# Second block's second mixer: latent projections ahead of the indexer, weight slabs split by quarters, and the last selection steps between attention steps

## The reference, cut to what matters

```python
def odd_mixer(x, w_in, q_norm_g, kv_norm_g, w_uq, w_ukv, w_o):
    qc, kc, vc, qi, ki, wi, cq, ckv, kr = split_cols(x @ w_in, ODD_SIZES)
    out_c = dsa_attention(qc, kc, vc, qi, ki, wi)          # 8 heads, 1 kv head
    q  = (rms_norm_2(cq, q_norm_g) @ w_uq)                 # rank 256 -> 8 x (64 + 32)
    kv = (rms_norm_2(ckv, kv_norm_g) @ w_ukv)              # rank 128 -> 8 x (64 + 64)
    ...                                                    # rope on q's and k's last 32
    out_d = causal_block_attention(q, k, kv[..., MLA_NOPE:])
    return jnp.concatenate([out_c, out_d], axis=-1) @ w_o
```

## Time and profile before

| | |
|---|---|
| median of 3 runs | 2633.47 us (2627.46 to 2636.49) |
| the profiled execution | 2608.53 us, its span 2606.3 us |
| mean granted TensorE clock in it | 0.949 of 2.4 GHz |
| PE busy | 2456.7 us, 94% of the span |
| DVE, ACT busy | 1716.4 us (66%), 1190.4 us (46%) |
| the mixer that is changed | from 2041 us to about 2240 us of the span |

### The profile page before, as it was taken

How to read it: one execution, slowest core, us unless ns; L and a number is a source line. 1 busy time by engine, 2 the same in 40 slices (tenths; PEclk the granted TensorE clock), 3 DMA queues, 4 the chain that set the end, 5 groups by cost and what they waited for, 6 DMA issues and landing times.

```text
span 2606.3 us, 33935 instructions
## 1 busy us (share of the span) xinstructions
PE 2456.7 (94%) x14244; PEld 2104.4 (81%) x14244; DVE 1716.4 (66%) x2226; ACT 1190.4 (46%) x1482; POOL 98.7 (4%) x187
## 2 busy tenths in 40 slices
PE   6999999898989999999999999899899879899998
PEld 2778887767789999998899988677778757778776
DVE  4897776654766656655466555587788653588786
ACT  3212222343544444445254444376576433476665
POOL 0111111010000000000000000000000000000000
PEclk8999999999999999999899998999999865999999
DMA  7677877322134544554344542287788310298774
GB/s 269 212 242 263 267 264 248 122 89 76 65 116 176 195 164 176 194 202 178 107 165 169 194 152 81 69 298 278 269 335 328 121 65 17 86 354 309 290 302 183
DMA packets 80385, 501.17 MB, mean 192 GB/s; under 512 B 9604, under 2 KB 10708, under 8 KB 28496
## 3 DMA queue, kind: packets, MB, share of 16 engines
q1 hardware_dynamic: 59120, 423.66, 44.4%
q0 software_dynamic: 21088, 75.01, 9.2%
HBM read 497.58 MB, written 1.05 MB: 191 GB/s over the span
## 4 chain that ended last, share of the span: by engine, by line
PE 69%; DVE 16%; ACT 9%; issue 4%; DMA 2%; DVEq 0%; SPq 0%; ACTq 0%
PE bank L394 67%; DVE wl L1896 7%; ACT wh L1301 6%; DVE macc L1929 2%; PE bank L577 1%; ACT s L1389 1%; DVE f L2054 1%; DMA raw<-in_wstream 1%; DVE s L2045 1%; PE bank L1198 1%; DMA raw<-in_wmod 1%; DVE rs L1953 1%; DVE hl L2029 0%; ACT H L1398 0%; ACT X L1624 0%
## 5 line engine op out<-in xcount | busy, mean ns | idle before, releaser
L1896 DVE TENSOR_TENSOR wl<-raw,wh 128x2048 fp32r<-128x2048 f32 x393 | 899.2, 2290 | 409.3 <-ACT wh L1301 407.2
L1301 ACT ACTIVATE wh<-raw 128x2048 fp32r<-128x2048 f32 x393 | 750.0, 1911 | 379.1 <-PE bank L394 363.3
L394 PE MATMUL bank<-hh,wh 128*128 128x258 f32 (+2 forms) x2200 | 703.8, 320 | 37.2 <-DVE wl L1896 18.8
L394 PE MATMUL bank<-hh,wl 128*128 128x258 f32 (+2 forms) x2200 | 683.7, 311 | 0.0
L394 PE MATMUL bank<-hl,wh 128*128 128x258 f32 (+2 forms) x2200 | 682.2, 310 | 0.0
L394 PEld LDWEIGHTS bank<-hh,wh 128*128 128x128 f32 x2200 | 430.7, 196 | 66.5 <-issue 19.0
L394 PEld LDWEIGHTS bank<-hl,wh 128*128 128x128 f32 x2200 | 431.2, 196 | 18.6
L394 PEld LDWEIGHTS bank<-hh,wl 128*128 128x128 f32 x2200 | 429.8, 195 | 19.0
L394 PE MATMUL bank<-wh,hh 128*128 128x512 f32 (+1 forms) x704 | 278.4, 395 | 5.1 <-DVE hl L2804 2.8
L394 PE MATMUL bank<-wl,hh 128*128 128x512 f32 (+1 forms) x704 | 274.1, 389 | 0.0
L394 PE MATMUL bank<-wh,hl 128*128 128x512 f32 (+1 forms) x704 | 273.8, 389 | 0.0
(11 more groups left out here) (424 smaller groups left out, 2709.8 us busy)
## 6 DMA issues: line engine op xcount, KB each, us to landing
raw<-in_wstream SPq DMA_DIRECT2D x393, 1024.0 KB, 4.9
mring<-in_wmod POOLq DMA_DIRECT2D x128, 512.0 KB, 4.6
raw<-in_wmod SPq DMA_DIRECT2D x8, 1024.0 KB, 9.7
X<-in_xT SPq DMA_DIRECT2D x1, 2048.0 KB, 12.6
bias<-in_nabias POOLq DMA_DIRECT2D x16, 128.0 KB, 2.5
c_sglg<-in_sglg POOLq DMA_DIRECT2D x1, 1024.0 KB, 5.0
c_sglb<-in_sglb POOLq DMA_DIRECT2D x1, 1024.0 KB, 7.4
out<-X SPq DMA_DIRECT2D x4, 256.0 KB, 2.2
```

The costliest lines, as they stand in the source:

```text
L394: return e.matmul(out, lhsT, rhs, start=start, stop=stop, skip_group_check=True)
L1301: e.activation(wh[i % NB][:], raw[i % NR][:], ACT.Copy).then_inc(*slab_high(i))
L1896: e.tensor_tensor(wl[i % NB][:], raw[i % NR][:], wh[i % NB][:].bitcast(F32), ALU.subtract).then_inc(*slab_low(i))
```

## The change

1. **Order of chunks.** The latents come first (`ocq`, `ock`), then `oki` (with `root_sum` inside), `oqi`, `ovw`; only then the selection starts, under `okr`, `oqc` and `okc`. The latents' norm on DVE and ACT moves ahead with them. `rotate` for the keys now stands inside the first `oqc` chunk, `rotate` for the queries one part later. ACT loads the table of the exponential right after the square root.
2. **Pumps.** Before attention 22 selection steps are taken on every engine (before: all 36). The other 14, DVE's own of qb 1, follow one by one behind the first attention steps.
3. **Quarters.** In this mixer (`st.fine`) a slab is split in four pieces of 128x512, each when PE begins four new tiles, and nine pieces ahead instead of twelve; under the `oqc` chunks a piece stands behind two or three attention steps instead of a whole slab ahead of five. PE still waits for a whole low part. Outside this mixer nothing moves.

```diff
@@ tensor_program
                         if k in units:
                             attend(1)
+                            pump(1)
...
-            p(1, 7, "oki")
+            p(2, 8, "ocq")
+            p(1, 10, "ock")
+            p(1, 7, "oki", middle=root_sum)
             p(2, 5, "oqi")
             project_tok("oin", 12, P, 2, h, dve_out, "ovw")
             st.selection = selection()
-            p(2, 8, "ocq", pumps=True)
-            p(1, 10, "ock", pumps=True)
-            p(1, 11, "okr", pumps=True, middle=root_sum)
+            p(1, 11, "okr", pumps=True)
...
-            pump(100)
             st.units = attention("od", OD, od.a, logits, values, (4,))
             p(3, 0, "oqc", m0=1, units=OD_UNITS)
             result.mark("h read", "oin")
+            pump(100)
@@ scalar_program
         def split_upto(n):
-            while st.split < min(n, len(order)):
-                i = st.split
+            while st.split < min(n, 4 * len(order)):
+                i, c = divmod(st.split, 4)
+                m = min(4 - c, n - st.split)
+                o = slice(512 * c, 512 * (c + m))
                 w.wait_ge(raw_in[i % NR], "slab", i)
                 if i >= NB:
                     w.wait_ge(result, "slab", i - NB)
-                e.activation(wh[i % NB][:], raw[i % NR][:], ACT.Copy).then_inc(*slab_high(i))
-                st.split += 1
+                e.activation(wh[i % NB][:, o], raw[i % NR][:, o], ACT.Copy).then_inc(*slab_high(st.split + m))
+                st.split += m
 
         def taken(n):
-            for i in range(-(-st.tile // TILES), -(-(st.tile + n) // TILES)):
-                split_upto(i + NB)
+            for i in range(-(-st.tile // 4), -(-(st.tile + n) // 4)):
+                if st.fine or i % 4 == 0:
+                    split_upto(i + 4 * NB - 3 if st.fine else i + 4 * NB)
             st.tile += n
...
                 e.activation(rs[:], rs[:], ACT.Sqrt).then_inc(*act_out("oroot"))
+                w.wait_ge(dve_out, "ones")
+                act(warm[:], ones[:, 0:1], ACT.Exp, key=("warm", "od"))
...
-                    taken(KC)
+                    for n in units:
+                        for _ in range(n):
+                            attend(1)
+                            pump(1)
+                        taken(4)
                     if pumps:
                         pump(4)
-                    attend(units)
...
-            pump(100)
             st.units = attention("od", OD, od.a)
-            p(3, "oqc", query, 0.125, m0=1, units=len(OD_UNITS))
+            p(3, "oqc", query, 0.125, m0=1, units=(2, 3))
+            pump(100)
@@ vector_program (its split_upto and taken change as ACT's do)
-            pump(100)
             st.units = attention("od", OD, od.a, logits, lambda g: heads_of(od.Y, g % 2, 512 if g < 2 else 0))
-            for _ in range(3):
-                taken(KC)
-                attend(len(OD_UNITS))
+            for n in 3 * (2, 3):
+                for _ in range(n):
+                    attend(1)
+                    pump(1)
+                taken(4)
+            pump(100)
```

More of the change, by code:

```diff
@@ L1292, in scalar_program @@
         st = Room()
-        st.tile, st.split, st.selection, st.units = 0, 0, iter(()), iter(())
+        st.tile, st.split, st.fine, st.selection, st.units = 0, 0, False, iter(()), iter(())
         def split_upto(n):
-            while st.split < min(n, len(order)):
-                i = st.split
+            while st.split < min(n, 4 * len(order)):
+                i, c = divmod(st.split, 4)
+                m = min(4 - c, n - st.split)
+                o = slice(512 * c, 512 * (c + m))
                 w.wait_ge(raw_in[i % NR], "slab", i)
@@ L1728, in query @@
                 return od.qc[:, m, :]
-            p(1, "oki", lambda m: od.ki[:])
-            p(2, "oqi", lambda m: od.qi[:, m, :], 0.125)
-            taken(KC)
-            st.selection = selection()
-            p(2, "ocq", lambda m: od.cq[:, m, :], pumps=True)
-            p(1, "ock", lambda m: od.cq[:, 2, :], pumps=True)
+            p(2, "ocq", lambda m: od.cq[:, m, :])
+            p(1, "ock", lambda m: od.cq[:, 2, :])
             for k in range(3):
@@ L1738, in odd_mixer @@
                 e.activation(od.lsq[:, k, :], od.cq[:, k, :], ACT.Square).then_inc(*act_out("osq", k))
-            p(1, "okr", lambda m: od.kr[:], pumps=True, middle=root)
-            p(1, "oqc", query, 0.125, pumps=True, middle=high)
+            p(1, "oki", lambda m: od.ki[:])
+            root()
+            p(1, "oqi", lambda m: od.qi[:, m, :], 0.125)
+            p(1, "oqi", lambda m: od.qi[:, m, :], 0.125, m0=1, middle=high)
+            taken(KC)
+            st.selection = selection()
+            p(1, "okr", lambda m: od.kr[:], pumps=True)
+            p(1, "oqc", query, 0.125, pumps=True)
             p(1, "okc", lambda m: od.kc[:], pumps=True)
@@ L1888, in vector_program @@
         st = Room()
-        st.tile, st.split, st.host, st.selection, st.units = 0, 0, False, iter(()), iter(())
+        st.tile, st.split, st.fine, st.host, st.selection, st.units = 0, 0, False, False, iter(()), iter(())
         mods = ModSums()
         def split_upto(n):
-            while st.split < min(n, len(order)):
-                i = st.split
-                w.wait_ge(slab_high, i)
-                e.tensor_tensor(wl[i % NB][:], raw[i % NR][:], wh[i % NB][:].bitcast(F32), ALU.subtract).then_inc(*slab_low(i))
-                st.split += 1
+            while st.split < min(n, 4 * len(order)):
+                i, c = divmod(st.split, 4)
+                m = min(4 - c, n - st.split)
+                o = slice(512 * c, 512 * (c + m))
+                w.wait_ge(slab_high, st.split + m)
+                e.tensor_tensor(wl[i % NB][:, o], raw[i % NR][:, o], wh[i % NB][:, o].bitcast(F32), ALU.subtract).then_inc(*slab_low(st.split + m))
+                if c + m == 4:
+                    slab_low.mark("slab", i)
+                st.split += m
         def taken(n):
-            for i in range(-(-st.tile // TILES), -(-(st.tile + n) // TILES)):
-                if st.host and i:
+            for i in range(-(-st.tile // 4), -(-(st.tile + n) // 4)):
+                if st.host and i and i % 4 == 0:
                     mod_sums()
@@ L2617, in odd_mixer @@
             taken(4 * KC)
-            w.wait_ge(result, "ovw")
-            for q in range(2):
-                e.tensor_copy(od.vw[:, q, :], banks[bank_of["ovw", q]][:, 0:P]).then_inc(*dve_out("ovw", q))
-            w.wait_ge(dve_out, "ovw", 1)
-            e.tensor_scalar(od.wi[:], od.vw[:, :, 64:68], 0.5, None, ALU.mult).then_inc(*dve_out("owi"))
-            st.selection = selection()
-            for _ in range(3):
-                taken(KC)
-                pump(4)
-            taken(KC)
-            pump(2)
             b = banks[bank_of["ossq",]]
@@ L2648, in odd_mixer @@
                 e.tensor_tensor(od.cl[:, k, :], od.cq[:, k, :], od.ch[:, k, :].bitcast(F32), ALU.subtract).then_inc(*dve_out("ocl", k))
-            pump(2)
+            taken(KC)
+            w.wait_ge(result, "ovw")
+            for q in range(2):
+                e.tensor_copy(od.vw[:, q, :], banks[bank_of["ovw", q]][:, 0:P]).then_inc(*dve_out("ovw", q))
+            w.wait_ge(dve_out, "ovw", 1)
+            e.tensor_scalar(od.wi[:], od.vw[:, :, 64:68], 0.5, None, ALU.mult).then_inc(*dve_out("owi"))
+            st.selection = selection()
+            taken(KC)
+            pump(4)
             def rotate(key, src):
```

32 lines of the change are left out of this document (18 added, 14 removed).

## The result

The changed kernel takes 2589.72 us, the median of 4 executions (2586.14 to 2601.8); the kernel before took 2634.49 us beside it (4 executions, 2627.46 to 2636.49). The ratio is 0.984 (95% interval 0.980 to 0.988), 45 us less. I had forecast 2618, with 2577 to 2628 as the range. The time lies in the range, but in the case "the clock holds for a part" (2576 to 2612, chance 0.22), not in the likeliest one (2610 to 2626). Two more comparisons of the same kernels gave 0.989 (0.983 to 0.994) and 0.987 (0.984 to 0.990).

A forecast was written before the change was run, and what follows sets the result against it. The changed mixer was taken as bound by PE at half clock in attention, and by waits before it. 14.4 + 3.5 - 1.5 - 1.0 = 15.4 us less, from 2633.5 to 2618; range 2577 to 2628.

The forecast's parts named there:

- the clock holds for a part: Changed mixer's attention: the clock falls somewhere on the way; 2576 to 2612 us, middle 2595, chance 0.22.
- Removed waits, 14.4 us: PE's waits for `o_cl` (2.1), `X` (2.4) and two for an exponential (4.9, 5.0) go: 14.4 us less.
- The stretch back at full clock, 3.5: Around 2085 to 2100 us, run at 0.83, 0.50 and 0.65, the clock should stay at 1.00: 3.5 us back.
- The wait at tile 100, 1.5: At the first tile of `oqc` chunk 1, PE waits 1.5 us for ACT's last ReLU; range 0 to 4.
- The price of a piece, 691 ns: A 128x512 piece on DVE, ahead of attention, costs what a same-shaped instruction took, 691 ns; 16 pieces make 9.8 us.
- The rival of dear pieces: Ahead of attention, 16 pieces at the whole-slab price of 2.29 us delay chunk 1: 11.5 us slower, 2645, chance 0.04.
- The cover within attention: DVE's added selection steps and pieces fit beside PE: 2.05 us of DVE in a PE step of 2.9.
- The rival of uncovered additions (2636): In attention, PE waits for every selection round and piece ahead of a unit on DVE: 17.6 us lost, chance 0.08.
- The size for a low clock, 15.4: Changed mixer with attention at 0.50: 14.4 + 3.5 - 1.5 - 1.0 = 15.4 us less.
- The forecast's clock: Changed mixer: the clock falls at attention's entry or first steps and stays at 0.50; 2618 us, chance 0.52.
- the second rival: In attention, the clock holds at first and falls somewhere on the way: 2576 to 2612 us, chance 0.22.
- the first, a clock that holds throughout: The clock stays full through the changed mixer's attention: 60 us less, 2573, chance 0.14.

The follow-up runs named there:

- hold: Changed kernel with six 128x512 copies on ACT ahead of the indexer's last ReLU, lengthening PE's wait at tile 100; 2624.09 us, ratio 1.002 to before.
- spread: Changed kernel with the last chunk's eight tiles spread over eight attention steps instead of five, leaving two steps without weight tiles; 2604.42 us, ratio 0.993 to before.
- fill_ds: Changed kernel with 42 useless products ahead of seven attention steps without weight tiles, and 40 ahead of the last ten units' logits; 2582.0 us, ratio 0.982 to before.
- whole: Changed kernel with slabs split whole instead of in quarters, still behind the steps; 2618.46 us, ratio 0.997 to before.
- fill: Changed kernel with six useless 128x256 products ahead of each of the seven attention steps without weight tiles; 2587.63 us, ratio 0.985 to before.

## Why the prediction was right or wrong

- **Removed waits, 14.4 us: right.** All four are gone, and tile 100 comes 96.6 us behind the start of the mixer in place of 103.5: 6.9 us earlier, where my numbers (2101.5 to 2095.0) make 6.5. The product that had waited 4.9 us for the first exponential comes 11.7 us earlier; I had said some 10.
- **The stretch back at full clock, 3.5: right.** It reads 1.00.
- **The wait at tile 100, 1.5: right**, 1.62, for the instruction named.
- **The price of a piece, 691 ns: right**, 688. The rival of dear pieces falls with it.
- **The cover within attention: right, also at full clock.** DVE's first eight units start at 2118.62 and the last of them at 2132.89, 2.04 us each; I had worked out 2.05. PE waits for an exponential only once, 0.7 us, after the last selection step. The rival of uncovered additions (2636) did not come.
- **The size for a low clock, 15.4: right.** hold is that case. Without its added 4.0 us its mixer is 243.8, 13.4 less than before.
- **The forecast's clock: wrong, and it is the step that failed.** That the time still lies in my range is owed to the second rival, not to the forecast. I wrote: "I expect it to fall at the entry or in the first steps, and to stay at 0.50 until attention ends." I judged by the length of idle times (1.1 and 1.2 survived, 2.1 and 2.2 not, mine of 1.5 between) and by the fact that the low clock did not rise in this mixture. The second is true and says nothing of whether a high one falls. The first was no measure. The wait of 1.6 was passed at 1.00 in all three profiles of the changed kernel. The wait of 1.17 us that I showed as survived is there in all 14 profiles, 1.17 to 1.18 us long, and in four of them the clock falls some 2 us behind it; in the changed kernel it reads 0.59 over 25 us. And in spread it fell with no wait near. The runs put in its place what PE does between the waits: in the changed kernel and in spread the fall comes where steps have few or no weight tiles, and with enough such work added (fill_ds) it does not come. The step is mis-sized by 42.2 - 13.4 = 28.8 us, and all of it lies between tile 100 and the fall: hold takes 70.3 us there and the changed kernel 41.3. That is 0.41 of the stretch, where I had chosen 0.45 for the rival; the second half, at 0.50 in both, gives nothing.
- **The second rival's size: near.** Its middle was 2595; 2587 to 2593 were measured.
- **The same difference taken from the median: right, with a reason that I lacked.** I found "no stretch that I can blame" for the 25 us between the profile of before and its median. Most of it is a stretch of the first block's mixer, 19 us between the two profiles of before, and low in 10 of 14 profiles. It lies outside the change, so that subtracting a mixer's difference from the median was sound; taking the profile's 2608.5 as typical was not.

The rule that I weighed said that only a longer idle gap brings a drop. By it the gap at tile 100 had to leave the clock at 2.4 GHz, and there the Trainium skill ("TensorE: Matmul & The Clock Gate", section "Why this matters for your kernels") was right and I was wrong. I had written that this is the second rival; without a longer gap in attention the rule leads to the first, a clock that holds throughout, and that did not come. For the whole of attention the rule does not agree: the granted clock fell in spread without any wait in the table, and in whole at one of 2.17 us; the measurement decides. The same page describes, in "A second HAM failure mode: psum-queue depth-cycling", a clock that goes to and fro because PE idles in small amounts between groups; whether attention's steps are such a case no run here shows.

The best kernel here is fill_ds: its mixer is 8 to 10 us shorter than those of the three profiles of the changed kernel. Its median is 2582.0 against 2587 to 2593, and the intervals of the ratios overlap, so that by the timed executions it is faster than before (0.982) and not surely faster than the changed kernel, whose repeats were timed on other chips. What stays open is where exactly the clock falls in a given execution: the fall came in three profiles of the same kernel within 4 us of the same place, with and without the wait for `Y` ahead of it, and in the first block it came or did not. Useful work in place of the filling was not tried, but for spread, which moved the tiles the wrong way.

## What to carry to other kernels

Where a profile shows a long stretch at half clock, ask first whether the engine enters it at full clock, and what real matrix work stands between its small products; a few microseconds of waiting removed ahead of it, or a few of products added within it, can be worth more than the stretch's own waits. Judge a change to such a place only with all its parts, since the parts one by one gave +6.9 and -6.8 us here and together -42. Compare two profiles product by product before trusting the difference of their spans: 28 us of luck in another layer hid two thirds of this gain.

## What the hardware showed that I had not expected

- The granted clock fell from 2.4 to 1.2 GHz with PE at work and without an idle time in the trace (spread, 2138.5 us), and held through idle times of 1.62 us at tile 100 and of 1.16 us for `Y` in fill and fill_ds.
- The same instruction stream with the same wait (1.17 and 1.18 us) was followed by a clock of 1.00 in one execution and 0.59 over 25 us in another; the clock fell behind it in 4 profiles of 14. A stretch of 44 us at 1.2 GHz in the first block is there in 10 profiles of 14. Executions of one kernel lie up to 38 us apart (2602.65 to 2640.85); such stretches account for 19 us between two profiles of the same kernel.
- Forty to eighty useless products made attention faster: 82 of them, 9.7 us of work at 0.118 us from one to the next, made the mixer 8.3 us shorter, and half as many, spread over the same steps, made it no shorter at all. 42 in the seven steps without weight tiles alone made it 3.1 us shorter.
